# All sixteen gate projections as pairs of the seven-product scheme, and three branch rows inside the last attention head

## What is computed

```python
gq, gk, gv, gr, ga, dq, dk, dv, gates = jnp.split(u @ w_in, ...)
ya = rmsnorm(gla(gq, gk, gv, ga, ...), ...) * jax.nn.silu(gr)
ya = ya.reshape(B, S, GLA_VW) @ w_branch_a           # 512 -> 1024
yb = rmsnorm(diff_attention(dq, dk, dv, ...), ...) * (1.0 - lam_init)
yb = yb.reshape(B, S, DIFF_VW) @ w_branch_b          # 512 -> 1024
g_a, g_b = jnp.split(jax.nn.sigmoid(gates), N_BRANCH, axis=-1)
return (g_a * ya + g_b * yb) @ w_out
```

## Time and profile before

| what | value |
|---|---|
| median of three executions | 2152.49 us (2150.22 to 2154.62) |
| the profiled execution | 2149.05 us, its span 2147.3 us |
| PE, matmul busy | 2109.5 us, 98% |
| PE, weight loads busy | 1733.7 us, 81% |
| DVE busy | 1358.4 us, 63% |
| POOL busy | 1393.4 us, 65% |
| ACT busy | 839.8 us, 39% |
| mean granted TensorE clock | 0.997 |

### The profile page before, as it was taken

One profiled execution on the slowest core, in us unless ns is written; L12 is line 12 of the kernel. 1 busy time (PEld: TensorE's weight loads), 2 busy tenths in 40 slices (PEclk: granted clock), 3 DMA queues, 4 the chain that ended last, 5 costly groups with the idle time before them and its releaser, 6 DMA issues.

```text
span 2147.3 us, 28195 instructions
## 1 busy us (share of the span) xinstructions
PE 2109.5 (98%) x10225; PEld 1733.7 (81%) x10225; DVE 1358.4 (63%) x2053; ACT 839.8 (39%) x1571; POOL 1393.4 (65%) x1096
## 2 busy tenths in 40 slices
PE   8999999999999999999999999999999999999998
PEld 7887777778878778888788888888787888888787
DVE  6966777778966821288566663534865444458956
ACT  7432222324445433344544453114423332244444
POOL 7888878878964777543321132336878877869953
PEclk9999999999999999999999999999999999999999
DMA  7245545558333323300111013411243333365333
GB/s 285 64 160 169 180 153 171 177 178 307 94 95 117 119 93 114 89 12 2 40 40 30 20 40 119 166 49 49 78 143 99 118 103 118 103 221 203 96 99 123
DMA packets 228619, 248.87 MB, mean 116 GB/s; under 512 B 10479, under 2 KB 155010, under 8 KB 228226
## 3 DMA queue, kind: packets, MB, share of 16 engines
q1 hardware_dynamic: 228338, 246.81, 35.3%
q10 hardware_dynamic: 144, 0.26, 0.0%
HBM read 191.98 MB, written 55.05 MB: 115 GB/s over the span
## 4 chain that ended last, share of the span: by engine, by line
PE 70%; DVE 10%; POOL 8%; DMA 5%; issue 3%; ACT 2%; SPq 1%; DVEq 0%; POOLq 0%; ACTq 0%
PE ps L2926 21%; PE ps L2801 16%; PE ps L3081 16%; PE ps L2937 5%; PE ps L2882 4%; DMA ada_half<-in_w_ada 3%; POOL w_lo L1221 3%; PE ps L3333 2%; PE ps L3298 1%; DVE x_op L2291 1%; DMA w_raw<-in_ffn_w_in 1%; DVE ada_acc L2101 1%; PE ps L3214 1%; PE ps L3318 1%; SPq L935 1%
## 5 line engine op out<-in xcount | busy, mean ns | idle before, releaser
L2926 PE MATMUL ps<-t,w_hi 128*128 128x512 f32 x1280 | 396.8, 391 | 7.2 <-DVE bufs L2314 4.0
L1221 POOL TENSOR_TENSOR w_lo<-w_raw,w_hi 128x512 fp32r<-128x512 f32 x240 | 356.0, 1495 | 50.2 <-ACT w_hi L1549 49.3
L3081 PE MATMUL ps<-x_op,w_hi 128*128 128x512 f32 x1208 | 373.8, 391 | 4.4 <-DVE x_op L2291 3.4
L1549 ACT ACTIVATE w_hi<-w_raw 128x512 fp32r<-128x512 f32 x240 | 142.2, 624 | 415.7 <-POOL w_raw L1307 176.6
L2926 PEld LDWEIGHTS ps<-t,w_hi 128*128 128x128 f32 x1280 | 238.9, 188 | 63.2 <-DVE bufs L2314 8.0
L3081 PEld LDWEIGHTS ps<-x_op,w_hi 128*128 128x128 f32 x1208 | 226.1, 188 | 55.4 <-POOL w_lo L1221 6.1
L1221 POOL TENSOR_TENSOR w_lo<-q,w_hi 128x512 fp32r<-128x512 f32 x132 | 199.1, 1518 | 98.0 <-ACT w_hi L1549 98.0
L1188 POOL TENSOR_SCALAR w_hi<-w_raw 128x1024 fp32r<-128x1024 f32 x41 | 45.0, 1097 | 323.1 <-PE ps L2801 267.8
L2926 PE MATMUL ps<-t,w_lo 128*128 128x512 f32 x640 | 249.5, 390 | 0.0
L3081 PE MATMUL ps<-x_op,w_lo 128*128 128x512 f32 x604 | 235.4, 390 | 0.0
L2291 DVE TENSOR_TENSOR x_op<-x_raw,x_op 128x512 fp32r<-128x512 f32 x154 | 178.4, 1169 | 84.7 <-ACT x_op L1559 83.8
(11 more groups left out here) (416 smaller groups left out, 4458.2 us busy)
## 6 DMA issues: line engine op xcount, KB each, us to landing
w_raw<-in_ffn_w_in SPq DMA_DIRECT2D x88, 512.0 KB, 4.3
hid_dram<-hid_raw SPq DMA_DIRECT2D x154, 256.0 KB, 5.2
x_raw<-hid_dram SPq DMA_DIRECT2D x154, 256.0 KB, 2.6
ada_half<-in_w_ada SPq DMA_DIRECT2D x112, 256.0 KB, 2.8
w_raw<-in_w_in SPq DMA_DIRECT2D x41, 512.0 KB, 3.6
q<-in_ffn_w_out SPq DMA_DIRECT2D x6, 1536.0 KB, 9.2
ada_full<-in_w_ada SPq DMA_DIRECT2D x16, 512.0 KB, 12.8
gate_dram<-h SPq DMA_DIRECT2D x12, 512.0 KB
```

What stands on the lines that cost most here:

```text
L1221: nc.gpsimd.tensor_tensor(lo, src, hi.bitcast(F32), ALU.subtract).then_inc(hs_ready, 1)
L1549: nc.scalar.activation(hs_place(n)[0], src, ACT.Copy).then_inc(wa_high, 1)
L2926: mm = nc.tensor.matmul(ps[bank][:], w[i], x[:, k, :], start=(first and k == 0 and q == 0), stop=(k == 3 and q == 2), skip_group_check=True)
L3081: mm = nc.tensor.matmul(ps[down_bank(p) + m][:], w[:, tile(m)], x_op[:, n % 3, x, :], start=(p in (0, 1, 3) and k == 0 and q == 0), stop=( ...
```

## The change

All 16 gates are made in the gate stage, as eight pairs (nine tiles with the value tile). No gate is projected in the attention or between the rows any more. In the last head, fills 2 to 7 are now the two halves of the rows (0,0), (0,1) and (0,2) of the branch product: 12 matmuls each into bank 0 (`filled`). For that the high and low parts of ya are made in steps 1 and 2 of the last head, by halves, in the space of u_hi (`high_ya`, `low_ya`), where they stood in steps 6 and 7 before. DVE, not ACT, takes a fill's result out of bank 0: it multiplies it by the gate that came back from DRAM (`fill_out`). The gates are all read from DRAM, 16 loads for 12, the first eight already in the last head. Behind the attention 13 rows are left, which use three pairs of banks in turn. The sixteen gate loads shift the slots of the later weight units (`mix_slot`). `u % SLOTS` became `mix_slot(u)` at all places, which the diff below leaves out, as it does the removed code of the sigmoids, the high and low parts before, and SP's old list.

```diff
-EARLY = 3
-_order = [("gate", 0, m) for m in range(EARLY)] + [("w", 0, 0), ("gate", 0, 3), ("w", 0, 1)]
-_order += [("w", _br, _i) for _br in range(2) for _i in range(0 if _br else 2, 4)]
-BRANCH_UNIT = {what: U_BRANCH + n for n, what in enumerate(_order)}
+FILLED = 3
+BRANCH_UNIT = {(br, i): U_BRANCH + 4 * br + i for br in range(2) for i in range(4)}
 MB = 0
-GATES = [(0, m) for m in range(EARLY + 1, KT)] + [(1, m) for m in range(KT)]
+GATES = [(br, m) for br in range(2) for m in range(KT)]
...
-        def y_places(places):
-            return [y_parts[:, j - 8, :] if j >= 8 else rar[:, j * S:(j + 1) * S] for j in places]
-        keep_r = keep_f[:].rearrange("p a b -> p (a b)")
-        y_b = [u_hi[:, j, KT - 2:KT, :].rearrange("p a b -> p (a b)") for j in range(2)]
-        y_hi = [y_places((0, 6, 8, 11)), [y_b[0], keep_r[:, 0:S]] + y_places((1, 4))]
-        y_lo = [y_places((2, 7, 9, 10)), [y_b[1], keep_r[:, S:2 * S]] + y_places((3, 5))]
+        def y_part(br, part, j, hf=None):
+            if br == 0:
+                return u_hi[:, hf, 4 * part + j, :]
+            row = ((0, 1, 4, 6), (2, 3, 5, 7))[part][j]
+            if hf is None:
+                return rar[:, row * S:(row + 1) * S]
+            return rar[:, row * S + hf * HALF:row * S + (hf + 1) * HALF]
...
-        staged += [staged[j] for j in (0, 1, 7, 3)]
+        STAGED_AGAIN = (0, 1, 2, 4, 5, 6, 7, 3)
+        staged += [staged[j] for j in STAGED_AGAIN]
...
-                return "gate", i % 2
+                return "branch", i % 2
...
+        def row_bank(br, m):
+            return (4, 6, 0)[(KT * br + m - FILLED) % 3]
+        def row_count(br, m):
+            return (KT * br + m) // 2 + 1 - (FILLED + 1) // 2
...
+        def mix_place(u):
+            return u if u < U_GV else u + len(GATES)
+        def mix_slot(u):
+            return mix_place(u) % SLOTS
...
+            for (br, i), u in BRANCH_UNIT.items():
+                wb = (a["w_branch_a"][0], a["w_branch_b"][0])[br]
+                slot = mix_slot(u)
+                sp.wait_ge(w_split, u - SLOTS + 1)
+                sp.dma_start(w_raw[:, slot, :].rearrange("p (k m) -> p k m", k=4),
+                             wb[:, 2 * P * i:2 * P * (i + 1)].rearrange("(k p) m -> p k m", p=P)
+                             ).then_inc(w_in_sem[slot], 16)
+                if (br, i) == (1, 0):
                     sp.wait_ge(gate_out, GATE_OUT + 16 * len(GATES))
+                    sp.wait_ge(fill_done, fill_count(DIFF_H - 1, 0))
                     for j in range(4):
                         gate_back(j)
-                if (what, br, i) == ("w", 1, 2):
+                    sp.wait_ge(unit_done, MB + r_unit(DIFF_H - 1) + 1)
                     for j in range(4, 8):
                         gate_back(j)
-            gate_back(8)
-            gate_back(9)
+                if (br, i) == (1, 2):
+                    for j in range(8, 11):
+                        gate_back(j)
+            gate_back(11)
             mix_columns(U_OUT, a["w_out"][0], 0)
-            gate_back(11)
-            sp.wait_ge(unit_done, BRANCH_UNIT["w", 0, 3] + 1)
-            sp.wait_ge(yhi_ready, 8)
-            sp.wait_ge(ylo_ready, 8)
+            for j in range(12, 16):
+                gate_back(j)
...
+                def high_ya(hf):
+                    act.wait_ge(rt_ready, 2 * (DIFF_H - 1) + hf + 1)
+                    for j in range(4):
+                        copy(y_part(0, 0, j, hf), ya[:, j, half(hf)], yhi_ready)
+                def high_yb(j):
+                    copy(y_part(1, 0, j), yb[:, j, :], yhi_ready)
...
+                        if hd == DIFF_H - 1 and i in (1, 2):
+                            high_ya(i - 1)
...
+                act.wait_ge(yb_ready, 2 * DIFF_H)
+                for j in range(4):
+                    high_yb(j)
+                high_z(range(KT))
...
+                        m = filled_row(i)
+                        gate_here(dve, GATES.index((0, m)))
+                        nc.vector.tensor_tensor(z[m][:, half(hf)], staged[m][:, half(hf)], ps[0][:],
+                                                ALU.mult).then_inc(zz_ready, 1)
...
+                def low_ya(hf):
+                    for j in range(4):
+                        dve.wait_ge(yhi_ready, 4 * hf + j + 1)
+                        low_part(y_part(0, 1, j, hf), ya[:, j, half(hf)], y_part(0, 0, j, hf), ylo_ready)
...
+                            low_ya(i - 1)
                         if i != 6:
...
-                    for m in range(KT):
+                    for m in range(0 if br else FILLED, KT):
                         if br == 0 and m >= 4:
...
+                        i = GATES.index((br, m))
+                        gate_here(dve, i)
                         for hf in range(2):
-                            n = 2 * KT * br + 2 * m + hf
-                            if (br, m) in GATES:
-                                i = GATES.index((br, m))
-                                gate_here(dve, i)
-                                sig = staged[i][:, half(hf)]
-                            else:
-                                dve.wait_ge(sig_ready, n + 1)
-                                sig = z[m][:, half(hf)] if m < EARLY else sig_b[hf]
-                            product = ps[4 - 4 * (m % 2) + hf][:]
+                            sig, product = staged[i][:, half(hf)], ps[row_bank(br, m) + hf][:]
...
+                def filled(i):
+                    m, hf = filled_row(i), i % 2
+                    if i == 2:
+                        pe.wait_ge(r_ready, 2 * DIFF_H)
+                    else:
+                        pe.wait_ge(zz_ready, i - 2)
+                    u = BRANCH_UNIT[0, m // 2]
+                    if m % 2 + hf == 0:
+                        pe.wait_ge(w_split, MB + u + 1)
+                    for k in range(4):
+                        if m == 0:
+                            pe.wait_ge(ylo_ready, 4 * hf + k + 1)
+                        mm = row_three(0, m, k, hf, ps[0])
+                    mm.then_inc(unit_done if completes(DIFF_H - 1, i) else fill_done, 1)
+                def row_three(br, m, k, hf, bank):
+                    slot = mix_slot(BRANCH_UNIT[br, m // 2])
+                    c = slice((2 * k + m % 2) * P, (2 * k + m % 2 + 1) * P)
+                    return three(bank[:], (w_hi[:, slot, c], w_lo[:, slot, c]),
+                                 (y_part(br, 0, k, hf), y_part(br, 1, k, hf)), k == 0, k == 3)
...
-                branch_product(0, 0)
-                pe.wait_ge(gate_kept, 2 * EARLY)
-                pe.wait_ge(yb_ready, 2 * DIFF_H)
-                pe.wait_ge(ob_ready, TT * DIFF_H)
-                branch_product(0, 1)
-                pe.wait_ge(sig_ready, 2 * EARLY - 2)
-                u = BRANCH_UNIT["gate", 0, EARLY]
-                project(MB + u, u % SLOTS, 2 + 4 * (EARLY % 2)).then_inc(unit_done, 1)
                 for br in range(2):
-                    for m in range(0 if br else 2, KT):
+                    for m in range(0 if br else FILLED, KT):
+                        if (br, m) == (0, FILLED + 2):
+                            pe.wait_ge(yb_ready, 2 * DIFF_H)
+                            pe.wait_ge(ob_ready, TT * DIFF_H)
                         branch_product(br, m)
...
                     if m == 1:
-                        pe.wait_ge(zz_ready, 4 * KT - 2)
-                    if m == 3:
                         pe.wait_ge(zz_ready, 4 * KT)
```

More of the change, by code:

```diff
@@ L1834, in fill_out @@
                     what, hf = fill_of(hd, i)
+                    if what == "branch":
+                        return
                     if completes(hd, i):
@@ L1844, in fill_out @@
                         nc.scalar.preload_act_table_set("natural_log_exp_and_others")
-                    elif what == "gate":
-                        if i == 6:
-                            act.wait_ge(rt_ready, 2 * DIFF_H)
-                        copy(z[i // 2 - 1][:, half(hf)], ps[0][:], gate_kept)
                     elif what == "v":
@@ L2685, in mixer @@
                             low_v(hd, i)
-                        if hd == DIFF_H - 1 and i >= 6:
-                            for j in (2 * i - 12, 2 * i - 11):
-                                low_y(0, j)
                         if i == 5 and hd + 1 < DIFF_H:
@@ L3235, in first_part @@
                         k = 2 * part + i
-                        mm = three(ps[1][:], (w_hi[:, u % SLOTS, tile(k)], w_lo[:, u % SLOTS, tile(k)]),
+                        mm = three(ps[1][:], (w_hi[:, mix_slot(u), tile(k)], w_lo[:, mix_slot(u), tile(k)]),
                                    (u_hi[:, hf, k, :], u_lo[:, hf, k, :]), k == 0, k == KT - 1)
@@ L3364, in fill @@
                         pe.wait_ge(r_ready, 2 * hd + i)
-                    elif what == "gate":
-                        pe.wait_ge(gate_kept, i - 2)
                     elif i in (3, 4):
@@ L3372, in fill @@
                         pe.wait_ge(dqlo, 4 * (hd + 1) + 3)
```

(4 more changed lines are left out.)

129 lines of the change are left out of this document (42 added, 87 removed).

## The result

The changed kernel took **2163.32 us** (median of 6 runs, 2161.00 to 2164.35), the kernel before 2150.59 us (median of 6, 2146.94 to 2154.62): ratio 1.0057, interval 1.0046 to 1.0068, **slower by 12.7 us**. The forecast was 2165.5, with a range of 2158 to 2173 and a chance of 0.88 for slower. The profiled execution of the changed kernel took 2164.35 (span 2162.6), that of before 2149.05 (span 2147.3). The two are 15.3 us apart, more than the medians, since single runs scatter: over 3.4 us for the changed kernel, 7.7 us for the one before.

A forecast was written before the change was run, and what follows sets the result against it. PE was taken to bound the kernel, busy 98%, but DVE to pace the last head once fills are short. 38.1 - 27.3 + 0.7 + 1.5 = +13.0 on a median of 2152.49 gave 2165.5 us, range 2158 to 2173.

The forecast's parts named there:

- Gate stage, +38.1: Gate stage: two more tiles of 19.05 us each, paced by PE, +38.1 us.
- Behind the attention, -27.3: Behind the attention: 13 rows and a turn, 71.1 us, replace 16 rows and a gate, 98.4 us; -27.3 us.
- The staged gates and the loads costed at nothing: Loads of staged gates from DRAM: issued some 20 us before the first is read, so no cost.
- The last head: DVE sets the pace, +0.7: Last head: short fills wait for DVE's multiplication at its step's end, so it ends 0.7 us later, not 16.5 earlier.
- Step 1: Last head, step 1: four low parts beside POOL's split, 2.2 us added; step 2 starts at 1256.8 instead of 1254.26.
- Steps 2 to 4: Last head: DVE's steps with the added multiplication, and low parts in step 2, start 9.5, 7.8 and 9.5 us apart.
- Step 5: Last head, step 5: DVE's step lasts 9.36 us, to 1293.1, counted without the POOL split.
- The clock, +1.5: Last head: PE's granted clock falls behind the wait of fill 6, +1.5 us; bounds nothing to 4.2.
- Rival A: Last head stays PE's with DVE's steps hidden, so -16.5 holds: -5.7 in all, 2146.8 us; chance 6%.
- Rival B: Last head: DVE's waits shrink, each step 1.3 us shorter than summed, -8: 2157 us; chance 6%.
- Rival C: Last head: PE's clock stays at 1.2 GHz from step 3 on, ending some 19 us later: 2184 us; chance 8%.
- the sum (+13.0): Whole kernel: gate stage 38.1, rows behind the attention -27.3, last head 0.7 and clock 1.5 add to +13.0 us.

The follow-up runs named there:

- e1: The kernel before with fills 2 to 7 of its last head cut to 12 matmuls each, nothing added to DVE: 2145.89 us, ratio 0.9974.
- e7: The changed kernel with no row in the last head, all 16 rows computed behind the attention: 2175.77 us, ratio 1.0112 to the kernel before.
- e4: The changed kernel with DVE's multiplication of a fill in steps 2 to 5 moved right behind its maxima: 2158.04 us, ratio 1.0032 to the kernel before.
- e5: e4 with ya's low parts in steps 1 and 2 behind DVE's maxima, ACT's copies before its exponentials: 2153.6 us, ratio 1.0007; measured again 2154.75, 1.0018.
- e3: The changed kernel with 12 extra matmuls on PE in the wait before fill 6 of the last head: 2162.54 us, ratio 1.0050 to the kernel before.

## Why the prediction was right, point by point

- **Gate stage, +38.1.** Measured 38.8 up to the end of step 1, the tile at 19.04. Right. Of the other 0.7, 0.2 stands ahead of the stage's tiles (785.54 to 785.76) and 0.5 between the stage's last addition (861.70, now 900.00) and the reciprocal of step 0, a stretch that scatters by far more between executions.
- **Behind the attention, -27.3.** Measured -27.2 (71.24 for a forecast of 71.1), without a wait of PE. Right. The staged gates and the loads costed at nothing cost nothing.
- **The last head: DVE sets the pace, +0.7.** Right in mechanism, shown three times: e1 (short fills alone give PE's waits), e7 (no fills at all, the same steps), and e4 and e5 (moves on DVE and ACT alone shorten the head by 11.5 us). In size it came out as +4.9 with the clock, where +0.7 and +1.5 were forecast. The 2.7 us between lie in single terms, the largest of them the clock and step 5. *Step 1:* four low parts beside POOL's split cost 5.5 us, not 4.6, and the step ended 0.6 late; the bound named (each of POOL's three pieces waited for, 3.6 over the 2.4) was nearer than the value taken. *Steps 2 to 4:* 9.65, 7.79, 9.20 for 9.52, 7.84, 9.54, together right to 0.3. *Step 5:* 10.45 for 9.36. The maximum, 0.17 before, took 1.27, beside POOL's split of a unit that row 1's second half had just released. I had counted POOL out of step 5 because its old split there had moved, and did not ask where the new one lands; only the top of the range had 2 us for it.
- **The clock, +1.5.** The stretch was where I put it, behind fill 6's wait, but it lasted for all of the fill: 5.3 us for 2.9 with the clock held up. It costs 2.6 at its place (e3), not 1.5. The cold stretch behind the 4.3 us wait at 1305.96 fell into DVE's time, as argued; e7 shows how far that goes. It did use up the wait that was forecast in front of fill 4: PE came to that fill at 1314.52, behind the multiplication of 1313.02.
- **Rival A** (the head stays PE's) falls with e1 and e7, and with it the ranking of engines by occupancy that was weighed against the rows. **Rival B** shortens the steps by 1.3; they were not shorter. **Rival C** does not occur in the changed kernel, whose clock is 1.00 again by 1314. The cold head of e7 costs little, since it is DVE's head by then; C's price assumed that PE's cold time would lie on the path.
- The forecast, 2165.5, is 2.2 us high though the trace's shift (+16.5 at the output projection) was larger than the sum (+13.0). Of the 2.2, 1.9 is the base: 2152.49 was the median of three runs of the kernel before, that of six is 2150.59. Against the median shift, +12.7, the sum was right to 0.3, which is partly luck: terms missed by 3.5 us, against which stand the 1.2 us behind the rows and the choice of executions: the profiled one of the changed kernel lies 1.0 above its median, that of before 1.5 below.
- PE's idle time in the head was forecast as some 17 us and is 13.2 as the list of waits has it. What is missing went into half-clocked matmuls, which count as busy.

Not shown: what the 1.2 us behind the rows are, and whether e3's 2.6 us at its place arrive in the whole time.

## What to carry to other kernels

Work that covers another engine's latency is worth what the other engine's step leaves open, step by step. Before half of it is taken away, write out the other engine's step with its waits; and when the cover gets thin, put each new consumer into that engine's own wait (here DVE's for ACT's exponentials), not at the step's end. The place of four multiplications and eight subtractions on DVE, with eight copies on ACT, was worth 8 to 11 us of the 13 that the change lost, with not one instruction less. And an average of idle time is no room: ask per wait what can be put in front of it.
